# Modulation vectors of a diffusion backbone: partition sums by VectorE and one fold per sweep, where TensorE summed every batch

## The chip, the cores and the metric

The kernel runs on one core of a Trainium2 chip. A core has a matrix engine (TensorE, PE in the profile), a vector engine (VectorE, DVE), a scalar engine (ScalarE, ACT), GpSimd (POOL) and SyncE (SP), which here issues all loads and stores. PEld is TensorE's loading of weights. The metric is the time on the device in microseconds, the median of several runs.

## What is computed

Two layers of a diffusion backbone over 512 latent tokens and 256 context tokens of width 1024, all in fp32. Every sub-layer is modulated by vectors made from the conditioning inputs `c` and `c_ctx`:

```
sc, scc = silu(c), silu(c_ctx)
for i in range(2):
    m  = split(sc  @ w_mod[i] + b_mod[i], 9)      # w_mod[i]: 1024 x 9216
    mc = split(scc @ w_mod[i] + b_mod[i], 9)
    h = h + 0.5 * m[2] * swiglu(modulate(rmsnorm(h), m[0], m[1]), w1, w3, w2)      # ffn1, D_FF = 2816
    n = modulate(rmsnorm(h), m[3], m[4])
    h = h + m[5] * token_mixing(n, ...)            # pooling, latent attention, differential attention
    h = h + 0.5 * m[8] * swiglu(modulate(rmsnorm(h), m[6], m[7]), w1, w3, w2)      # ffn2
    # the context stream hc likewise with mc (its mixing and ffn2 in the first layer alone)
return rmsnorm(h)
```

## The kernel before

**Sweeps.** All large matmuls run in "sweeps" of units (`plan_sweeps`). A unit has two slots s = 0, 1; each slot is one 128-column tile of weights, split by ACT (`hi_w`, L811) and DVE (`lo_w`, L1070, `split_lo`) into a high and a low part, and three matmuls per 128-row tile of the input (hi x hi, hi x lo, lo x hi, L563) over 768 tokens, in pieces of 512 and 256. An `_up` sweep has 11 units over 8 input tiles (w1 in slot 0, w3 in slot 1), a `_down` sweep 4 units over 11 input tiles. Each feed-forward part is up, down, up, down (arg 0, 0, 1, 1); between ffn1 and ffn2 stand five `in` sweeps, the mixer and an `out` sweep. Each slot has one buffer for its raw, high and low weights, so DVE can split the next weights of a slot only when PE has finished the slot's last unit (`unit_done`); PE waits for `lo_ready`. At the start of an `_up` sweep with arg 0 and of the first `in` sweep (`starts_norm`) the normed input is made tile by tile by DVE and ACT (`norm_x`), and PE runs both slots of unit 0 together as the tiles come.

**Modulation vectors.** The first 16 tiles of 128 modulation columns are made by PE in the prologue. The other 128 are made beside the feed-forward sweeps: one *batch* of two tiles (`MOD_T`) per unit, in the eight up and down sweeps of layer 0 and in the first down sweep of layer 1 (11 or 4 batches each, 64 in all). SP loads 1 MB of `w_mod` per batch into `mod_w` (`load_mod`, after the last batch's sums). DVE (`mod_add`, L1165) multiplies each of the 8 row tiles of 256 columns by one value of silu(c) per partition, for c and for c_ctx, and adds them up in `mod_acc` (128 x 512, two streams of 256): 2 TENSOR_SCALAR (L1175) and 14 SCALAR_TENSOR_TENSOR (L1178). What is left is a sum over the 128 partitions. PE does it (`mod_tiles`, L569): four matmuls per batch with a 128 x 128 part of `mod_acc` as weights and a tile of ones as the moving side, into `pair[2]` in PSUM, after every unit. DVE takes one column of each of the results, adds the bias and writes `mod` (`mod_evict`, L1182, two instructions of 2 columns at L1188) in the next pass. `gate` (L1358) and the shift and scale of the norms are read from `mod`.

**Order.** It is written out by hand: each engine has one stream of instructions, and semaphores join them. In one pass of an up loop DVE runs: split slot 0, product of slots 0 and 1 (L1141) and its low part (L1144), split slot 1, evict, next batch. PE runs slot 0, slot 1, `mod_tiles`.

## Time and profile before

| | us |
|---|---|
| time, median of 3 runs | 3199.53 (3188.82 to 3199.97) |
| profiled execution: span from first to last instruction | 3194.2 |
| PE busy | 3027.5 (95%) |
| DVE busy | 1519.1 (48%) |
| ACT busy | 875.4 (27%) |
| share of the chain that ended last: PE / DVE / ACT | 88% / 5% / 4% |

The files of this kernel give the span of the profiled execution and the times of three runs; no time beside the span is listed for the profiled execution itself. The median of the runs is 5.3 us above the span. The chain is followed back from the last instruction: at each step to what released it, or to the instruction before it on its engine. Of the page, the chain says what bounds the kernel and the groups by line say what an operation takes; the timelines give the order in a stretch, with the idle time before an instruction in brackets and what ended it. Ends of matmuls are modelled, so the step from one start to the next is the better measure of their pace. PE clock is given as a share of 2.4 GHz; it has two levels, 1.2 and 2.4 GHz.

### The profile page before, as it was taken

How to read it: one execution, taken by the hardware profiler on the slowest of the kernel's cores; microseconds unless marked ns; L12 is line 12 of the kernel's file. 1: busy time of each engine (PE TensorE's matmuls, PEld its weight loads, DVE VectorE, ACT ScalarE, POOL GpSimd, SP SyncE). 2: the span in 40 equal slices, each digit the busy share in tenths (PEclk: the TensorE clock that was granted, in tenths of full speed). 3: DMA queues.
4: the chain of work that ended last, by engine and by line, in shares of the span. 5: the costliest groups of instructions: out<-in, count | busy, mean ns of one | idle time of the engine just before them, and what ended most of it. 6: DMA issues, size and time to landing. Idle time of an engine off the chain costs nothing.

```text
span 3194.2 us, 41772 instructions
## 1 busy us (share of the span) xinstructions
PE 3027.5 (95%) x16066; PEld 2495.7 (78%) x16066; DVE 1519.1 (48%) x2542; ACT 875.4 (27%) x1174; POOL 109.1 (3%) x82
## 2 busy tenths in 40 slices
PE   7999999989879889999999899999989889899998
PEld 3888888878647578888888788888868647678886
DVE  4665465541377447555565523422242376443333
ACT  3221121131346732111121312112131246432222
POOL 0000000000340000000000000000000230000000
PEclk9999999999999999999999999999999989999999
DMA  5434334312200023442433122312213200123332
GB/s 187 125 112 131 101 112 132 98 41 66 59 0 1 6 68 106 124 123 89 124 117 114 40 66 82 96 57 61 70 48 74 65 1 1 58 74 103 88 99 72
DMA packets 421951, 254.62 MB, mean 80 GB/s; under 512 B 25729, under 2 KB 417513, under 8 KB 421866
## 3 DMA queue, kind: packets, MB, share of 16 engines
q1 hardware_dynamic: 421866, 253.46, 26.7%
q8 instruction: 57, 0.93, 0.1%
q14 instruction: 28, 0.23, 0.0%
HBM read 251.34 MB, written 2.10 MB: 79 GB/s over the span
## 4 chain that ended last, share of the span: by engine, by line
PE 88%; DVE 5%; ACT 4%; issue 2%; DMA 0%; SPq 0%; DVEq 0%; ACTq 0%
PE pair L563 76%; PE pair L671 3%; PE pair L743 2%; PE pair L576 2%; PE pair L692 1%; PE pair L497 1%; DVE buf L1123 1%; PE pair L675 1%; ACT buf L957 1%; DVE n_lo L1114 1%; DVE proj L1234 1%; ACT L830 1%; PE pair L654 1%; DVE buf L1233 0%; DMA pro_w<-in_w_mod 0%
## 5 line engine op out<-in xcount | busy, mean ns | idle before, releaser
L563 PE MATMUL pair<-n_hi,hi_w 128*128 128x512 f32 (+1 forms) x3224 | 911.8, 352 | 51.7 <-DVE n_lo L1114 42.7
L563 PE MATMUL pair<-n_lo,hi_w 128*128 128x512 f32 (+1 forms) x3224 | 905.4, 350 | 0.0
L563 PE MATMUL pair<-n_hi,lo_w 128*128 128x512 f32 (+1 forms) x3224 | 904.0, 349 | 0.0
L563 PEld LDWEIGHTS pair<-n_hi,hi_w 128*128 128x128 f32 x3224 | 516.3, 190 | 141.6 <-issue 49.2
L1070 DVE TENSOR_TENSOR lo_w<-raw_w,hi_w 128x1024 fp32r<-128x1024 f32 (+1 forms) x296 | 387.9, 1311 | 484.3 <-ACT hi_w L811 480.4
L563 PEld LDWEIGHTS pair<-n_hi,lo_w 128*128 128x128 f32 x3224 | 515.9, 189 | 87.0
L563 PEld LDWEIGHTS pair<-n_lo,hi_w 128*128 128x128 f32 x3224 | 516.2, 190 | 86.5 <-issue 0.2
L811 ACT CAST hi_w<-raw_w 128x1024 fp32r<-128x1024 f32 (+1 forms) x296 | 329.0, 1112 | 406.3 <-PE pair L563 402.7
L1178 DVE SCALAR_TENSOR_TENSOR mod_acc<-mod_w,silu_c,mod_acc 128x256 f32<-128x256 f32 x896 | 360.4, 483 | 0.0
L563 PE MATMUL pair<-h_hi,hi_w 128*128 128x512 f32 x1232 | 343.7, 349 | 0.0
L563 PE MATMUL pair<-h_lo,hi_w 128*128 128x512 f32 x1232 | 342.1, 347 | 0.0
L563 PE MATMUL pair<-h_hi,lo_w 128*128 128x512 f32 x1232 | 341.9, 347 | 0.0
L1141 DVE TENSOR_TENSOR buf<-pair,buf 128x768 f32<-128x768 f32 (+1 forms) x88 | 78.4, 891 | 404.8 <-PE pair L563 404.8
L1160 DVE SCALAR_TENSOR_TENSOR x<-pair,gate,x 128x512 f32 (+3 forms) x136 | 82.0, 638 | 351.6 <-PE pair L563 351.2
L866 ACT CAST h_hi<-buf 128x768 f32 (+3 forms) x88 | 68.9, 783 | 608.4 <-DVE buf L1141 608.4
L563 PEld LDWEIGHTS pair<-h_hi,lo_w 128*128 128x128 f32 x1232 | 195.2, 188 | 32.5
L563 PEld LDWEIGHTS pair<-h_lo,hi_w 128*128 128x128 f32 x1232 | 195.1, 188 | 32.5
L563 PEld LDWEIGHTS pair<-h_hi,hi_w 128*128 128x128 f32 x1232 | 195.1, 188 | 31.5
L862 ACT ACTIVATE buf<-pair 128x768 f32<-128x768 f32 (+1 forms) x88 | 66.8, 759 | 475.0 <-PE pair L563 475.0
L823 ACT ACTIVATE buf<-x 128x768 f32 (+3 forms) x56 | 43.8, 784 | 375.1 <-DVE x L1160 373.2
L1282 DVE TENSOR_REDUCE neg_max<-pair 128x1 f32<-128x768 f32 (+1 forms) x120 | 101.7, 850 | 88.0 <-PE pair L675 54.0
L957 ACT ACTIVATE buf<-pair,neg_max 128x768 f32<-128x768 f32 (+1 forms) x120 | 97.0, 811 | 125.9 <-PE pair L692 66.0
(157 smaller groups left out, 1940.9 us busy)
## 6 DMA issues: line engine op xcount, KB each, us to landing
raw_w<-in_ffn_w SPq DMA_DIRECT2D x176, 512.0 KB, 3.7
mod_w<-in_w_mod SPq DMA_DIRECT2D x64, 1024.0 KB, 5.0
raw_w<-in_ffn_w SPq DMA_DIRECT2D x64, 704.0 KB, 4.6
raw_w<-in_w_in SPq DMA_DIRECT2D x38, 512.0 KB, 3.8
pro_w<-in_w_mod SPq DMA_DIRECT2D x2, 4096.0 KB, 19.0
raw_w<-in_w_out SPq DMA_DIRECT2D x16, 512.0 KB, 3.8
x_tok<-in_x SPq DMA_DIRECT2D x4, 512.0 KB, 5.4
out<-x_tok SPq DMA_DIRECT2D x4, 512.0 KB, 2.7
```

What stands on the lines that cost most here:

```text
L563: mm = pe.matmul(pair[s][:, a:a + m], wt[:, k * P:(k + 1) * P], tile(src, k, m, a), start=(n == 0 and wt is hi and src is src_hi), stop=(n ...
L576: mm = pe.matmul(pair[2][:, (2 * m + e) * P:(2 * m + e + 1) * P], mod_acc[:, e * MOD_W + m * P:e * MOD_W + (m + 1) * P], ones[:, :], start ...
L671: mm = pe.matmul(pair[s][:, a:a + m], tile(proj, T_DQ + h, P, q0), tile(k_odd, h, m, k0 + a) if s else tile(proj, T_DK + h, m, k0 + a), st ...
L811: act.copy(hi_w[s][:, 0:w["kt"] * P], raw_w[s][:, 0:w["kt"] * P]).then_inc(hi_ready[s], 1)
L862: act.activation(act_buf[:, 0:width(w, 0)], pair[0][:, 0:width(w, 0)], ACT.Silu)\
L866: act.copy(tile(h_hi, i, width(w, 1)), hid_buf[:, 0:width(w, 1)]).then_inc(hhi_ready, 1)
L957: act.activation(buf[step_buf(L, n) + (s if kind == "diff" else 0)][:, 0:nk], pair[s][:, 0:nk], ACT.Exp, bias=neg_max[:, c % 8:c % 8 + 1], ...
L1070: dve.tensor_tensor(lo_w[s][:, 0:m], raw_w[s][:, 0:m], hi_w[s][:, 0:m].bitcast(F32), ALU.subtract)\
L1141: dve.tensor_tensor(hid_buf[:, 0:m], pair[1][:, 0:m], act_buf[:, 0:m], ALU.mult)\
L1160: ins = dve.scalar_tensor_tensor(out=xs, in0=pair[s][:, a:a + m], scalar=gate[:, bass.ds((2 * i + s) * 2 + e, 1)], in1=xs, op0=ALU.mult, o ...
L1178: ins = dve.scalar_tensor_tensor(out=acc, in0=part, scalar=gain, in1=acc, op0=ALU.mult, op1=ALU.add)
L1282: dve.tensor_reduce(neg_max[:, c:c + 1], pair[s][:, 0:nk], AX.X, ALU.max, negate=True)\
```

## The change

The sum over partitions is made in two steps. After each batch DVE reduces `mod_acc` with one `tensor_reduce` that transposes blocks of 32 x 32 as it reads (`apply_transpose`): within each group of 32 partitions every column is summed, and column 32 j + q of the 512 lands in partition q of the group, column j of 16, in `mod_part`. The four groups are added by PE once per sweep (`mod_fold`): `fold` holds four 32 x 32 unit matrices on top of each other and is the weight tile of four matmuls, whose moving side is every fourth column of `mod_part` (44 columns after an up sweep, 16 after a down sweep) and whose outputs go to partitions 0, 32, 64 and 96 of `pair[2]`. The fold of a sweep stands in the next sweep, behind slot 0 of its unit 0, or behind both slots where the sweep starts with a norm. DVE's evict is one pair of instructions per sweep, at the same place, ahead of that sweep's first batch; `gate` is made behind it. `mod_part` has two buffers, used in turn. Four small loads on SP fill `fold`, ahead of the two prologue loads of `w_mod`. Nine folds take the place of 64 times four matmuls.

```diff
@@ SP @@
+            for g in range(4):
+                sp.dma_start(fold[32 * g:32 * (g + 1), :], t["k_ident"][0:32, 0:32]).then_inc(fold_full, 16)
@@ PE @@
-            def mod_tiles(w, i):
-                b = cnt["batch"] + i
-                pe.wait_ge(mod_sum, 2 * KD * b)
-                pe.wait_ge(mod_out, b)
-                for m in range(MOD_T):
-                    for e in range(2):
-                        mm = pe.matmul(pair[2][:, (2 * m + e) * P:(2 * m + e + 1) * P],
-                                       mod_acc[:, e * MOD_W + m * P:e * MOD_W + (m + 1) * P], ones[:, :],
-                                       start=True, stop=True)
-                mm.then_inc(mod_done, 1)
+            def mod_fold(w):
+                pe.wait_ge(fold_full, 16 * 4)
+                pe.wait_ge(mod_folded, cnt["batch"])
+                pe.wait_ge(mod_out, cnt["mod"])
+                n = w["n"]
+                for j in range(4):
+                    mm = pe.matmul(pair[2][32 * j:32 * (j + 1), 0:2 * MOD_T * n], fold[:, :],
+                                   mod_part[cnt["mod"] % 2][:, j:8 * MOD_T * n:4], start=True, stop=True)
+                mm.then_inc(mod_done, 1)
+                cnt["mod"] += 1
-            def sweep(w):
-                per = mod_tile(w) is not None
+            def sweep(w, before):
                 if starts_norm(w):
                     unit(w, 0, (0, 1), True)
                 else:
                     unit(w, 0, (0,), True)
+                if before is not None and mod_tile(before) is not None:
+                    mod_fold(before)
+                if not starts_norm(w):
                     unit(w, 0, (1,), True)
-                if per:
-                    mod_tiles(w, 0)
                 if w["n"] > 1:
                     with pe.Fori(1, w["n"]) as i:
                         unit(w, i, (0,), False)
                         unit(w, i, (1,), False)
-                        if per:
-                            mod_tiles(w, i)
@@ DVE @@
             def mod_add(w, i):
...
-                dve.wait_ge(mod_done, b)
+                    dve.wait_ge(mod_folded, b)
...
+                dve.wait_ge(mod_sum, 2 * KD * (b + 1))
+                at = i * (8 * MOD_T)
+                dve.tensor_reduce(mod_part[cnt["mod"] % 2][:, bass.ds(at, 8 * MOD_T)],
+                                  mod_acc[:, :].rearrange("p (j f) -> p j f", f=32), AX.X, ALU.add,
+                                  apply_transpose=True).then_inc(mod_folded, 1)
-            def mod_evict(w, i):
...
+            def mod_evict(w):
+                n, u = w["n"], mod_tile(w)
+                dve.wait_ge(mod_done, cnt["mod"] + 1)
...
+                for e in range(2):
+                    ins = dve.tensor_tensor(cols_of[:, :, :, e], sums[:, :, e, :], bias, ALU.add)
                 ins.then_inc(mod_out, 1)
             def sweep(q):
...
                 if not starts_norm(w):
                     split_lo(w, 0, 1)
+                if q and mod_tile(SWEEPS[q - 1]) is not None:
+                    mod_evict(SWEEPS[q - 1])
+                if w["arg"] == 0 and w["what"] in ("ffn1_down", "ffn2_down", "out"):
+                    make_gate(w)
                 if ends_step(w):
                     clear_x()
                 if per:
                     mod_add(w, 0)
                 finish(w, 0, 0)
                 if w["n"] > 1:
                     with dve.Fori(1, w["n"]) as i:
...
                         if per:
-                            mod_evict(w, i - 1)
                             mod_add(w, i)
```

On DVE, at the hand-over from the first up sweep to the first down sweep of layer 0, the kernel before has (a row is a line, operation, output <- inputs and shape; brackets name the semaphores it waits for):

```order
L1070 TENSOR_TENSOR lo_w<-raw_w,hi_w 128x1408 [waits hi_ready0]
L1141 TENSOR_TENSOR buf<-pair,buf 128x768 [waits h_ready,pair_free0,unit_done1]
L1144 TENSOR_TENSOR h_lo<-buf,h_hi 128x768 [waits hhi_ready]
L1188 TENSOR_SCALAR mod<-pair,b_mod 128x2 [waits mod_done]
L1188 TENSOR_SCALAR mod<-pair,b_mod 128x2
L1358 TENSOR_SCALAR gate<-mod 128x16 [waits mod_out]
L1070 TENSOR_TENSOR lo_w<-raw_w,hi_w 128x1408 [waits hi_ready1,dve_chain]
L1175 TENSOR_SCALAR mod_acc<-mod_w,silu_c 128x256 [waits mod_done,mod_full]
L1175 TENSOR_SCALAR mod_acc<-mod_w,silu_c 128x256
L1178 SCALAR_TENSOR_TENSOR mod_acc<-mod_w,silu_c,mod_acc 128x256 [waits mod_sum] x14
L1160 SCALAR_TENSOR_TENSOR x<-pair,gate,x 128x512 [waits unit_done0]
L1160 SCALAR_TENSOR_TENSOR x<-pair,gate,x 128x256
```

The changed kernel has there, with its own line numbers (4 to 20 higher):

```order
L1148 TENSOR_TENSOR h_lo<-buf,h_hi 128x768 [waits hhi_ready]
L1074 TENSOR_TENSOR lo_w<-raw_w,hi_w 128x1408 [waits hi_ready1]
L1202 TENSOR_TENSOR mod<-pair,b_mod 128x22 [waits mod_done]
L1202 TENSOR_TENSOR mod<-pair,b_mod 128x22
L1209 TENSOR_SCALAR gate<-mod 128x16 [waits mod_out]
L1180 TENSOR_SCALAR mod_acc<-mod_w,silu_c 128x256 [waits mod_folded,mod_full,dve_chain]
L1180 TENSOR_SCALAR mod_acc<-mod_w,silu_c 128x256
L1183 SCALAR_TENSOR_TENSOR mod_acc<-mod_w,silu_c,mod_acc 128x256 [waits mod_sum] x14
L1189 TENSOR_REDUCE mod_part<-mod_acc 128x16 [waits mod_sum]
L1164 SCALAR_TENSOR_TENSOR x<-pair,gate,x 128x512 [waits unit_done0]
L1164 SCALAR_TENSOR_TENSOR x<-pair,gate,x 128x256
```

The evict and the gate have moved from ahead of the weight split to behind it, and the `mod_done` that they wait for is now that of PE's fold in this sweep; the reduction stands behind the batch.

On PE, at the end of the loop body of the first up sweep, the kernel before has

```order
L563 MATMUL pair<-n_hi,lo_w 128x512
L563 MATMUL pair<-n_hi,lo_w 128x256
L572 REGISTER_ALU
L576 MATMUL pair<-ones,mod_acc 128x128 [waits mod_out,mod_sum]
L576 MATMUL pair<-ones,mod_acc 128x128 x3
L591 REGISTER_ALU
L591 COMPARE_AND_BRANCH
```

and the changed kernel, first there and then between slot 0 and slot 1 of unit 0 of the first down sweep:

```order
L569 MATMUL pair<-n_hi,lo_w 128x512
L569 MATMUL pair<-n_hi,lo_w 128x256
L597 REGISTER_ALU
L597 COMPARE_AND_BRANCH
```

```order
L569 MATMUL pair<-h_hi,lo_w 128x512
L569 MATMUL pair<-h_hi,lo_w 128x256
L582 MATMUL pair<-mod_part,fold 32x44 [waits mod_out,mod_folded,fold_full]
L582 MATMUL pair<-mod_part,fold 32x44 x3
L569 MATMUL pair<-h_hi,hi_w 128x512 [waits h_ready,pair_free1,lo_ready1]
```

The four matmuls of every pass are gone, and four with 32 output partitions stand once between the two slots.

## Rows read from the trace of the kernel before

**Rows 1.** The page's chain that ended last, shares by engine.

```profile
PE 88%; DVE 5%; ACT 4%; issue 2%; DMA 0%; SPq 0%; DVEq 0%; ACTq 0%
```

**Rows 2.** The chain in order of time (start us, us, what): an up and a down pass.

```profile
121.76 0.89 PE pair L576 x8
122.65 16.96 PE pair L563 x96
...
558.56 23.32 PE pair L563 x132
```

**Rows 3.** The same view: first up sweep of layer 1, which makes no vectors.

```profile
1813.26 194.68 PE pair L563 x1092
```

**Rows 4.** Timeline (start us, us, engine, line, what, count [idle before]): one up pass.

```profile
108.13 0.34 DVE L1188 TENSOR_SCALAR mod<-pair,b_mod 128x2 f32 x2
...
121.59 1.05 PE L576 MATMUL pair<-ones,mod_acc 128*128 128x128 f32 x8
121.88 0.96 DVE L1141 TENSOR_TENSOR buf<-pair,buf 128x768 f32<-128x768 f32 x1 [5.56 <-PE pair L563]
```

**Rows 5.** Groups by line: records, busy us, mean ns, idle before.

```profile
L576 PE MATMUL pair<-ones,mod_acc 128*128 128x128 f32 x512 | 67.6, 275 | 2.6 <-DVE mod_acc L1178 2.6
```

**Rows 6.** Timeline of DVE: last update of x ahead of the mixer's norm.

```profile
654.53 1.14 DVE L1160 SCALAR_TENSOR_TENSOR x<-pair,gate,x 128x512 f32<-128x512 f32 x2 [6.17 <-PE pair L563]
```

**Rows 7.** Timeline of PE: eight small transposes of the prologue.

```profile
58.82 0.65 PE L505 MATMUL pair<-ident,mod_rows 2*128 2x2 f32 x8 [0.72 <-DVE mod_rows L1096]
```

**Rows 8.** Timeline of PE in the mixer: weights of 128 and of 64 columns.

```profile
1013.02 1.50 PE L743 MATMUL pair<-proj,v_tok 128*128 128x128 f32 x12
1014.36 1.46 PE L675 MATMUL pair<-proj 96*128 96x512 f32 x4
...
1022.65 1.52 PE L743 MATMUL pair<-proj,v_mla 128*64 128x128 f32 x12
1024.10 1.56 PE L675 MATMUL pair<-proj 96*128 96x512 f32 x4
```

**Rows 9.** Groups by line with shapes kept apart: reductions on DVE.

```profile
L1282 DVE TENSOR_REDUCE neg_max<-pair 128x1 f32<-128x768 f32 x96 | 91.5, 957 | 77.1 <-PE pair L675 45.1 <-PE pair L671 31.9
L1282 DVE TENSOR_REDUCE neg_max<-pair 128x1 f32<-128x256 f32 x24 | 10.1, 422 | 10.9 <-PE pair L675 8.9 <-PE pair L671 1.5
```

**Rows 10.** Timeline of DVE: start of the first down sweep.

```profile
269.43 0.61 DVE L1175 TENSOR_SCALAR mod_acc<-mod_w,silu_c 128x256 f32<-128x256 f32 x2
269.96 5.63 DVE L1178 SCALAR_TENSOR_TENSOR mod_acc<-mod_w,silu_c,mod_acc 128x256 f32<-128x256 f32 x14
277.11 1.14 DVE L1160 SCALAR_TENSOR_TENSOR x<-pair,gate,x 128x512 f32<-128x512 f32 x2 [1.52 <-PE pair L563]
278.52 1.63 DVE L1070 TENSOR_TENSOR lo_w<-raw_w,hi_w 128x1408 fp32r<-128x1408 f32 x1 [0.27 <-ACT hi_w L811]
```

**Rows 11.** Timelines of DVE, then PE: first up sweep, behind its norm.

```profile
79.88 5.63 DVE L1178 SCALAR_TENSOR_TENSOR mod_acc<-mod_w,silu_c,mod_acc 128x256 f32<-128x256 f32 x14
85.42 1.22 DVE L1070 TENSOR_TENSOR lo_w<-raw_w,hi_w 128x1024 fp32r<-128x1024 f32 x1
...
85.56 1.16 PE L576 MATMUL pair<-ones,mod_acc 128*128 128x128 f32 x8 [1.41 <-DVE mod_acc L1178]
86.69 0.62 PE L563 MATMUL pair<-n_hi,hi_w 128*128 128x512 f32 x2
```

**Rows 12.** PE timeline behind the mixer's norm; busy times of 688:690 (PEclk fourth figure).

```profile
686.89 0.61 PE L563 MATMUL pair<-n_hi,hi_w 128*128 128x512 f32 x2 [2.04 <-DVE lo_w L1070]
...
690.99 0.52 PE L563 MATMUL pair<-n_lo,hi_w 128*128 128x512 f32 x2
...
688.00:690.00 2.00, 2.00 (x8) 0.50 0.93 257
```

**Rows 13.** Timeline of SP's queue; busy times of 10:11 (last two: DMA share, GB/s).

```profile
10.66 0.25 SPq L363 DMA_DIRECT2D lam_row<-in_diff_lambda  x1
...
10.00:11.00 1.00, 0.00 (x0) 1.00 1.00 410
```

## What I predict

> **What bounds the kernel now.** I read the chain that ended last first, then the same chain in order of time, then the timelines of TensorE (PE) and VectorE (DVE) where one sweep hands over to the next. PE holds 88% of the chain [rows 1], so a PE instruction inside a sweep costs its full pace. The chain in order of time says so directly: in an up sweep the 96 matmuls of one loop pass take 16.96 us, then the eight L576 records take 0.89 us, then the next pass starts; a down pass is 23.32 us with the same 0.89 us behind it [rows 2]. (An fp32 matmul leaves two records, so 8 records are the four matmuls of a batch.) What a pass costs without them is in the same kernel: the first up sweep of layer 1 makes no modulation vectors, and its 1092 records run as one piece of 194.68 us [rows 3], which is 17.1 us per 96, a few slow ones at its start included. So nothing else is waiting right behind PE there: without L576 a pass of 16.96 us is to be had. DVE has room: after its last weight split in an up pass it sits idle for 5.56 us until PE ends its unit [rows 4].
>
> **The matmuls that go.** L576 has 512 records [rows 5], 8 per batch, so 64 batches. Not all lie on the path. The last batch of a `_down` sweep with arg 1 in layer 0 (two of them) is followed by a norm, which hangs on DVE and ScalarE (ACT); DVE's last update of x there starts when L563 ends, not when L576 does [rows 6], so nothing is gained. The first batch of the two sweeps that begin with a norm and make vectors (the first up sweep, and `ffn2_up` arg 0 of layer 0) is costed below from its own rows. The other 60 are on the path: 60 x 0.89 = **53.4 us gained**.
>
> **The folds that come.** Nine, one per sweep with batches, each four matmuls with 32 weight columns and 44 or 16 moving columns, 8 records. Two of them (at the start of `in` arg 0 of layer 0 and of the first up sweep of layer 1) fall where PE is idle anyway; seven are on the path. No such matmul is in the trace. From above: 8 full-size records, 0.89 us [rows 2]. From below: PE's smallest fp32 work, eight transposes, takes 0.65 us [rows 7]; less is possible if the four overlap, down to about 0.3, half of that, by estimate. On top, PE changes from a 128-column to a 32-column layout and back. The nearest rows are 12 records with 64-column weights, which take 1.45 us from their start to the next group's where the same 12 with 128 columns take 1.34 [rows 8]: 0.11 for a change, 0.22 for both. I take 0.65 + 0.22 = 0.9 us, near the smallest work because the moving side is short; the range is 0.3 to 1.2. **7 x 0.9 = 6.3 us back** (2.1 to 8.4).
>
> The Trainium skill speaks against the change here: "TensorEngine Tiling (Array Packing)", Key Properties, says that changing the tiling mode drains TensorE. The same section says that tiles can load and multiply in parallel. The rows show only the 0.11 us for a change to 64 columns; if the drain were hidden and the four tiles ran at once the folds would cost about 2 us in place of 6.3.
>
> **The new reduction on DVE.** Each batch gets one TENSOR_REDUCE of 128x512 to 128x16 that transposes 32x32 blocks as it reads. Plain reductions take 957 ns for 768 columns and 422 for 256 [rows 9], so 1.045 ns a column and 0.69 us for 512. A transposing one is not in the trace. From below the 0.42 us of 256 columns; from above twice the slope plus the fixed part, about 1.3, and I keep 2.0 as the far bound. I take 0.69, since the number of columns read is what the rows scale with. In the loop it is free: the old evict of two instructions (0.34 us) goes [rows 4], and 5.56 us of idle time cover the rest.
>
> The Trainium skill, "Vector Engine (DVE) Microarchitecture Reference", section 3.8, says of the transposing front end that it is "pipelined to sustain one element per cycle per lane", which would leave 0.69 as it is. "VectorE: DVE Perf Modes", in its closing table, calls tensor_reduce the slowest DVE op on a hot path. No row here shows it transposing.
>
> **Sweep starts: a new wait on DVE.** In a sweep that follows one with batches, DVE now waits for PE's fold, which stands after slot 0 of unit 0, and only then makes its first batch. Queued behind that wait are the batch, the x update in a down sweep, and the split of slot 0's next weights, for which PE waits after slot 1. Before, the batch ran under slot 0. Worked out from the moment the fold ends: 0.28 us until DVE starts (L1141 starts at 121.88, PE's unit had ended at 121.6, where L576 starts [rows 4]), evict 0.34, the batch from its first to its last instruction 6.15 (269.43 to 275.59 [rows 10]), the reduction with its wait 0.75, then
> - up sweeps (two in layer 0): split 1.22 [rows 11]. Sum 8.7 us against slot 1's 16.96 / 2 = 8.48: PE is late by about 0.25, **0.5 us for both**.
> - down sweeps (four): x update 1.14 and split 1.63 [rows 10], gate and waits 0.3. Sum 10.6 against 23.32 / 2 = 11.66: **0**, with 1 us to spare, less where x_sum is cleared first. With a reduction of 2 us the ups would be late by 1.6 each and the downs by 0.3 to 1.
>
> SyncE's load of the next modulation weights waits for the same batch, so it is issued later by about one unit, and so is the batch that needs it. The fifth down sweep with batches, that of layer 1, has no fold ahead and stays as it is; the up sweep behind it has a fold and no batch, so nothing is queued there but the evict.
>
> **The two norm starts with a batch.** PE waited until the batch was summed, ran L576 from 85.56 and resumed at 86.69, with DVE's split running beside it [rows 11]. Now PE resumes after batch, reduction and split: 79.88 + 5.63 = 85.51, + 0.75, + 1.22 = 87.5 us, that is 0.8 later. At the second place DVE has a little more cover; with 0.5 there, by estimate, **1.3 us come back.** PE is now idle for some 3 us there, where it had been idle 1.41 us before a filler. Where this kernel leaves PE idle for 2.04 us before a resumption, the granted clock is at half (0.50 of full, 1.2 in place of 2.4 GHz) soon after: from 686.89 to 690.99 seven groups of two matmuls take 4.10 us in place of 7 x 0.353 = 2.47 [rows 12, 2]. So I add 1.6 us at both places: **3.2 us back.**
>
> **The two norm starts with a fold.** PE's 2.04 us of idle time [rows 12] now holds the fold. But DVE's evict waits for it and stands ahead of the weight split that PE waits for. PE stops at 684.85 (686.89 - 2.04), so the fold ends at 685.7, and with 0.28 + 0.34 DVE is free at 686.3; the split began at 686.89 - 0.05 - 1.22 = 685.6. With the fold queued close behind the last unit I take **0.6 each, 1.2 us back.** I leave the clock as it was there.
>
> **Four small loads at the start** of `fold` stand ahead of the two 4 MB loads on SP's queue. An issue of such a load is 0.25 + 0.05 us, four make 1.2 us at most. The DMA engines were busy for all of that time (share 1.00 from 10 to 11 us) [rows 13], so most of it is hidden behind the queue; between 0 and 1.2 I take **0.6 us back**.
>
> **Sum.** 53.4 - 6.3 - 0.5 - 1.3 - 3.2 - 1.2 - 0.6 = 40.3 us. The profiled execution spans 3194.2 us; the median of the runs, 3199.53, is 5.3 us above, about what lies around the span. 3194.2 - 40.3 = 3153.9 in the profile, and 3199.5 - 40.3 = **3159.2 us** as time.
>
> **Rivals.**
> - *The handovers cost more.* The reduction takes 2 us and the clock also falls at the ups and at two of the downs. Up starts +2 x 1.3, norm starts +2 x 1.3, downs +4 x 0.6, four more falls of the clock +6.4, folds at 1.2 us +2.1, loads +0.6: 16.7 us, so 3176. For it: DVE at an up start is late already by my sum. Against: a PE wait of 1.41 us did not bring the clock down. Chance 0.14.
> - *They cost less.* Folds at 0.3 us (-4.2), no fall of the clock at the norm starts with a fold because the fold breaks up the idle time (-3.2), none from the loads (-0.6): 3151. Chance 0.18.
> - *The other side: the transposing reduction is slow.* Its place is every up pass (40 inside the loops). The cover is 5.56 us plus the 0.34 of the old evict less the 0.89 by which the pass shortens, so it decides from about 5 to 5.5 us; below that only the starts pay. With R us the loss is 40 x (R - 5.5) in the loops and 8 x (R - 0.7) at starts, if all of them pay; it outruns the gain of 40 by another 0.5% (16 us) at R = 5.9. At R = 7 it is 60 + 50 us: 3269. For it: no row shows a transposing read. Against: 5.9 us would be eleven times the slope of plain reductions. Chance 0.03.
> - *The gain is taken by another wait*, so that the change doesn't buy what the removed matmuls cost: the 1 MB load per batch comes later than the shorter passes ask for and DVE, then PE, wait for it, by 0.5 us or more of the 0.89 in each of some 60 passes: about 3190. Against: traffic has room, and the sweep without batches runs at the full pace. Chance 0.05.
>
> **How the numbers follow.** Forecast 0.60 (3150 to 3170), cheaper handovers 0.18, dearer 0.14, gain taken 0.05, slower 0.03. A difference of under 0.5% (16 us) is what a measurement of this kernel can't tell from none; only the last two cases fall short of it. Faster 0.92, same 0.05, slower 0.03. The range takes in both handover cases and, below, that the three runs themselves reach 10.7 us under their median: 3142 to 3177.
>
> **What the new profile would show.** Chain in order of time: up passes of 16.96 us back to back with no piece between (right), or a short DVE piece in each (reduction too slow). The group of the fold: 72 records, the step over it about 0.9 us. The reduction's own mean, 0.7 us. DVE's wait for PE before the evict at seven starts, near 10 us or less each, and at up starts a PE wait for lo_w of 0.2 to 0.5 us. At the two norm starts with a batch PE resumes some 3 us after it stopped and at half clock. If the time is above 3177, one of these is off by several times its size.

## The result, and the profile after

| | before | changed |
|---|---|---|
| time, median (us) | 3199.11 | 3138.28 |
| runs | 4 | 4, 3134.65 to 3144.0 |
| span of the profiled execution (us) | 3194.2 | 3134.9, its time 3136.8 |

The ratio is 0.9819, 95% interval 0.9801 to 0.9837: 61 us less. The forecast was 3159.2 us with a range of 3142 to 3177, so the direction was right and the time lies 3.7 us below the range. Span against span, 59.3 us went where 40.3 were expected. (What lies around the span is 3136.8 - 3134.9 = 1.9 us, not the 5.3 that the prediction put down to it; the profiled execution of before was a little under its median. The forecast was counted from the median, so this shifts nothing.) The other 19 us are what this part of the document looks for.

The page's chain that ended last, and from the groups by line and the table of waits the two new operations and DVE's new wait (waits: us in total, times, longest):

```profile
PE 86%; DVE 6%; ACT 4%; issue 2%; DMA 0%; SPq 0%; ACTq 0%; DVEq 0%
...
L582 PE MATMUL pair<-mod_part,fold 128*32 128x16 f32 (+1 forms) x72 | 2.7, 221 | 0.0
...
L1189 DVE TRANSPOSE_TENSOR_REDUCE mod_part<-mod_acc 128x512 f32 (+1 forms) x64 | 45.6, 712 | 8.5 <-DVE mod_acc L1183 4.7
...
DVE mod L1202 <- PE pair L582: 56.4, 9, 7.2
```

Against [rows 1] the picture is the same, PE a little less and DVE a little more. The 512 records of L576 [rows 5] are gone; 72 of L582 stand in their place. The reduction takes 0.712 us, where 0.69 was predicted from plain reductions [rows 9].

Now DVE's timeline in the first up sweep (start us, us, line, what), to be read against [rows 4], where L1141 was the same instruction as L1145 here:

```profile
106.69 0.96 DVE L1145 TENSOR_TENSOR buf<-pair,buf 128x768 f32<-128x768 f32 x1 [5.37 <-PE pair L569]
...
117.08 0.71 DVE L1189 TRANSPOSE_TENSOR_REDUCE mod_part<-mod_acc 128x512 f32 x1
...
123.44 0.96 DVE L1145 TENSOR_TENSOR buf<-pair,buf 128x768 f32<-128x768 f32 x1 [4.54 <-PE pair L569]
...
140.19 0.96 DVE L1145 TENSOR_TENSOR buf<-pair,buf 128x768 f32<-128x768 f32 x1 [4.55 <-PE pair L569]
```

From one L1145 to the next is a pass: 16.75 us. A pass of before was 16.96 + 0.89 = 17.85 [rows 2]. So 1.10 us went per pass, and not 0.89: the 96 matmuls themselves take 0.21 us less than they did. No edit touches them. That is the first sign of what the prediction lacked, and the second is in the last part of the kernel, where no vectors are made at all. There the granted clock is full, PE is never idle, and the number of matmul records in 100 us (in brackets) is a direct reading of their pace. First the kernel before, then the changed one:

```profile
2950.00:3050.00 100.00, 100.00 (x430) 1.00 0.30 86
```

```profile
2950.00:3050.00 100.00, 100.00 (x438) 1.00 0.34 99
```

430 and 438 records of 512 columns: 233 and 229 ns each. The new program runs old instructions faster.

### The profile page after: what moved, and what is told of

Read it like the earlier page. It is cut to its first block, busy times and chain, and to the rows that moved or that the text cites. A ratio compares the mean times of both kernels' runs of the same rounds, so it can differ in the third digit from the quotient of the medians.

```text
span 3134.9 us, 40610 instructions
## 1 busy us (share of the span) xinstructions
PE 2957.6 (94%) x15626; PEld 2440.8 (78%) x15626; DVE 1538.9 (49%) x2496; ACT 874.9 (28%) x1174; POOL 108.5 (3%) x82
## 4 chain that ended last, share of the span: by engine, by line
PE 86%; DVE 6%; ACT 4%; issue 2%; DMA 0%; SPq 0%; ACTq 0%; DVEq 0%
PE pair L569 77%; PE pair L675 3%; PE pair L747 2%; PE pair L696 1%; PE pair L503 1%; PE pair L679 1%; DVE buf L1127 1%; ACT buf L961 1%; DVE n_lo L1118 1%; ACT L834 1%; DVE mod_acc L1183 1%; DVE proj L1255 1%; PE pair L658 1%; DVE buf L1254 1%; ACT L837 0%
## 5 line engine op out<-in xcount | busy, mean ns | idle before, releaser
L569 PE MATMUL pair<-n_hi,hi_w 128*128 128x512 f32 (+1 forms) x3224 | 903.5, 350 | 57.3 <-DVE n_lo L1118 42.7
L569 PE MATMUL pair<-n_lo,hi_w 128*128 128x512 f32 (+1 forms) x3224 | 901.8, 349 | 0.0
L569 PE MATMUL pair<-n_hi,lo_w 128*128 128x512 f32 (+1 forms) x3224 | 897.5, 347 | 0.0
L569 PEld LDWEIGHTS pair<-n_hi,hi_w 128*128 128x128 f32 x3224 | 515.2, 190 | 143.7 <-issue 51.8
L569 PEld LDWEIGHTS pair<-n_lo,hi_w 128*128 128x128 f32 x3224 | 518.6, 190 | 82.8 <-issue 0.2
L569 PEld LDWEIGHTS pair<-n_hi,lo_w 128*128 128x128 f32 x3224 | 515.6, 189 | 82.1
L569 PE MATMUL pair<-h_hi,hi_w 128*128 128x512 f32 x1232 | 341.4, 347 | 2.2 <-DVE lo_w L1074 2.2
L569 PE MATMUL pair<-h_lo,hi_w 128*128 128x512 f32 x1232 | 341.3, 346 | 0.0
L569 PE MATMUL pair<-h_hi,lo_w 128*128 128x512 f32 x1232 | 339.4, 345 | 0.0
L1145 DVE TENSOR_TENSOR buf<-pair,buf 128x768 f32<-128x768 f32 (+1 forms) x88 | 78.4, 891 | 356.6 <-PE pair L569 356.6
L569 PEld LDWEIGHTS pair<-h_lo,hi_w 128*128 128x128 f32 x1232 | 196.1, 188 | 31.6
L569 PEld LDWEIGHTS pair<-h_hi,hi_w 128*128 128x128 f32 x1232 | 194.8, 188 | 33.0 <-issue 2.8
L569 PEld LDWEIGHTS pair<-h_hi,lo_w 128*128 128x128 f32 x1232 | 195.0, 188 | 31.4
```

Of the source, the lines that this page charges most:

```text
L569: mm = pe.matmul(pair[s][:, a:a + m], wt[:, k * P:(k + 1) * P], tile(src, k, m, a), start=(n == 0 and wt is hi and src is src_hi), stop=(n ...
L1145: dve.tensor_tensor(hid_buf[:, 0:m], pair[1][:, 0:m], act_buf[:, 0:m], ALU.mult)\
```

## Experiments: chance or address

"Pace" is here the step from the start of one large matmul, or of one pair, to the next. Two theories for its change. **Chance**: an execution of any of these programs falls into one pace or the other. **Address**: the change puts `fold`, 32 columns of fp32 or 128 bytes, into SBUF behind `ones`, and everything allocated behind it lies 128 bytes higher, the moving operands `n_hi`, `n_lo`, `h_hi` and `h_lo` too. `n_hi` began at byte 112192 of its partition, and begins at 112320 in the changed kernel. The weights (`hi_w`, `lo_w`) and `x` are allocated ahead of `fold` and stay where they were. (The expectations name a third theory, **code**: where the matmul stream is disturbed decides the pace. The runs on addresses below test it too, since they leave every instruction as it is.)

The two programs once more, unedited (before_again, after_again):

> The kernel before, unchanged, profiled once more. It asks whether the pace of the large matmuls is a property of the program or of the single execution. In the first profile of the kernel before every sweep steps at 353.3 ns per pair (a piece of 512 and one of 256 columns) and at 233.2 ns per 512-column matmul in the last sweeps; in the changed kernel some sweeps step at 349 ns and the last ones at 228.8 ns. Theory ADDRESS (the buffer of 32 columns moved all later buffers) and theory CODE (where TensorE's stream is disturbed decides which of two paces it falls into): 353.3 and 233.2 again, ratio 1.000. Theory CHANCE (an execution falls into one pace or the other): some sweeps at 349 or 228.8 ns, and a time between 3185 and 3200 us.

Measured: 3198.92 us (ratio 1.0006, interval 0.9995 to 1.0016), the slow pace in every sweep.

> The changed kernel, unchanged, profiled once more. Theories ADDRESS and CODE: the same pattern of paces by sweep as in its first profile (349 ns per pair in the first up and down sweep, in the `in` sweeps and in two up sweeps of layer 0, 228.8 ns in the last sweeps), ratio 0.981. Theory CHANCE: another pattern; the time moves with it by up to 10 us.

Measured: 3138.92 us (ratio 0.9815, 0.9798 to 0.9832); the fast pace again wherever only 512 columns are computed. In the sweeps of 512 and 256 columns the pattern was another one: from its first matmul to that of the next sweep, the second up sweep of layer 0 took 184.85 us where the first execution had 186.84, and the third 193.95 where it had 191.86. There chance does have a part, and this was not expected by the theory of addresses as it was written down.

Then the addresses alone. In the kernel before, one line more, a buffer that nothing uses (before_shift):

```diff
         ones = sb("ones", P)
+        gap = sb("gap", 32)
         mod = sb("mod", DEPTH * UNITS_MOD * 2)
```

> The kernel before with one unused buffer of 32 columns where the change puts its fold matrix, so that every later buffer lies at the addresses of the changed kernel; nothing else differs. Theory ADDRESS: the last sweeps step at 228.8 ns and some earlier ones at 349 ns per pair, and the time falls by 9 to 20 us, ratio 0.994 to 0.997. Theories CODE and CHANCE: no systematic difference from before, ratio 1.000 within 0.002.

Measured: 3180.11 us (ratio 0.9942, 0.9924 to 0.996). Some 16.6 us for a line that computes nothing. And in the changed kernel, the shift taken out while everything else stays (after_noshift):

```diff
-        fold = sb("fold", 32)
         mod = sb("mod", DEPTH * UNITS_MOD * 2)
...
         h_lo = sb("h_lo", FG * TOK, F32R)
+        fold = sb("fold", 32)
```

> The changed kernel with the fold matrix allocated behind all other buffers, so that these lie where they lay before. Theory ADDRESS: every sweep steps at 353.3 and 233.2 ns as before, and the time is 3138 + 19 = 3157 us, ratio 0.987. Theories CODE and CHANCE: 3138 us within 5, ratio 0.981, with sweeps at 349 and 228.8 ns.

Measured: 3153.45 us (ratio 0.9861, 0.9844 to 0.9878), inside the predicted range. Every sweep is back at the slow pace. Two rows of DVE's timeline, one pass apart, and the count of the last part:

```profile
125.18 0.96 DVE L1145 TENSOR_TENSOR buf<-pair,buf 128x768 f32<-128x768 f32 x1 [4.76 <-PE pair L569]
142.14 0.96 DVE L1145 TENSOR_TENSOR buf<-pair,buf 128x768 f32<-128x768 f32 x1 [4.77 <-PE pair L569]
```

```profile
2950.00:3050.00 100.00, 100.00 (x431) 1.00 0.32 93
```

The pass is 16.96 us, exactly what [rows 2] promised. So chance and code are out as the cause of the difference between the two programs, and the change has two parts: the announced one, worth 43.3 us (3196.75, measured beside it, to 3153.45), and one that nobody intended, the move of the buffers, worth 14.5 us (3153.45 to 3138.92). By the sweeps' lengths in the two profiled executions, 6.7 of the 16.8 us between them lie in sweeps of 512 columns alone, where the pace follows the address every time; nearly all of the rest lies in the other sweeps, where it does not.

**Whose address?** In shift_h `fold` stands between `n_lo` and the buffers behind it, so that only `h_hi`, `h_lo` (and `proj`) are moved:

```diff
         n_lo = sb("n_lo", KD * TOK, F32R)
+        fold = sb("fold", 32)
```

> The changed kernel with `fold` placed between `n_lo` and the buffers behind it: `h_hi` and `h_lo` (moving operands of the down sweeps) and `proj` lie 128 bytes higher than before the change, as in the changed kernel; `n_hi`, `n_lo` (moving operands of the up, in and out sweeps), `rstd`, `buf0` to `buf3` and the small vectors lie as before the change. Theory, each matmul's pace goes by the address of its own moving operand: in layer 1 the two ffn2 down sweeps step at 228.8 ns and the ffn2 up and out sweeps at 233.2; of the 16 us that the full shift brought here only 2 to 6 us come, 3147 to 3151.5 us. Rival A, one of the buffers in front (the outputs or inputs of DVE and ACT) matters: then no sweep is faster, 3153.5 us. Rival B, the pace of all sweeps hangs on something that h_hi, h_lo or proj share: all at 228.8, near 3138 us.

Measured: 3154.51 us (ratio 0.9867, 0.9851 to 0.9884), 3 us above the range that was expected. The pace answers the question better than the time does. Records in 50 us of the first ffn2 down sweep of layer 1 (moving operands `h_hi`, `h_lo`), first after_noshift, then this kernel:

```profile
2886.00:2936.00 50.00, 50.00 (x216) 1.00 0.31 91
```

```profile
2886.50:2936.50 50.00, 50.00 (x220) 1.00 0.32 93
```

and of this kernel 100 us of the up sweep behind it (moving `n_hi`, `n_lo`), with the same columns:

```profile
2950.00:3050.00 100.00, 100.00 (x430) 1.00 0.31 90
```

The down sweep took the fast pace and the up sweep did not. So for the down sweeps it is the address of `h_hi` and `h_lo` that counts, and `rstd`, the vectors and the other buffers in front of `n_hi`, which stayed, have no part in it; nor does it matter where the up sweep's results are written, since it writes `h_hi` and `h_lo` and stayed slow. For the up sweeps no run moves `n_hi` and `n_lo` without the buffers in front of them, so that it is their own moving operand there too is likely, but not shown. Since the weights never moved, the address itself and the distance from the weights can't be told apart either.

**Which addresses?** More unused columns behind `fold`, in the changed kernel: `gap = sb("gap", 16)` in gap16, 48 in gap48.

> The changed kernel with an unused buffer of 16 columns behind `fold`: everything from `mod` on lies 192 bytes higher than before the change (the changed kernel: 128). The start of `n_hi` modulo 256 bytes was 64 before, is 192 in the changed kernel, and is 0 here. Theory, the pace gets better with the alignment of the moving operand's start: the 512-column sweeps step at 228.8 ns or less and all 768-column sweeps at the faster of their two paces (349 in place of 353.3 ns for a pair): 12 us under the changed kernel, near 3127 us. Rival, it is the address bit of 128 bytes, or distance to another buffer, and not alignment: the time is that of the changed kernel, 3138 us, or, where 192 is as bad as 0, 3153 us.

Measured: 3136.01 us (ratio 0.9811, 0.9794 to 0.9827).

> The changed kernel with 48 unused columns behind `fold`: `n_hi` and the other moving operands start at 128 modulo 256 bytes (before the change 64, changed kernel 192, with 16 columns 0). Theory A, the distance to the next 256-byte boundary matters through the middle of the three paces that were seen: as 0, a step of 232.2 ns in the 512-column sweeps and 350.9 a pair in the others, 3136 us. Theory B, the address bit of 128 decides: as in the changed kernel 228.8 ns, 3138 us or less. Theory C: as before the change, 233.2 and 353.3 ns, 3153 us.

Measured: 3130.6 us (ratio 0.9785, 0.9769 to 0.98). The same 100 us in both:

```profile
2950.00:3050.00 100.00, 100.00 (x432) 1.00 0.34 98
```

```profile
2950.00:3050.00 100.00, 100.00 (x443) 1.00 0.35 102
```

| start of the moving operands modulo 256 bytes | 64 (before) | 0 (16 columns) | 192 (changed kernel) | 128 (48 columns) |
|---|---|---|---|---|
| ns a step, 512-column matmuls | 233.3 | 232.4 | 228.9 | 226.7 |
| time, changed kernel (us) | 3153.5 | 3136.0 | 3138.3, 3138.9 | 3130.6 |

The steps are the length of the last up sweep of layer 1 (123.20, 122.69, 120.85 and 119.68 us) by its 528 records. My theory for gap16, that rounder alignment is better, fell: 0 is the second slowest in the 512-column sweeps. Of gap48's three theories B comes nearest: the two starts in the upper half of 256 bytes, 128 and 192, are the quick ones, and 0 and 64 the slow ones; but it is not the same pace within a half. Four starts are too few for a rule. In the 768-column sweeps things are less simple. A pass of an up sweep is 48 pairs of matmuls (512 and 256 columns), so its length gives the pair. With a start at 0 it is 16.85 us, 351 ns a pair, and with 64 it is 16.96, 353 ns, in every sweep. With 192 it is 16.96 or 16.75 (349 ns), and which of them differs from execution to execution of one program. Here are two passes of the second up sweep of layer 0 in the changed kernel, and two in after_again:

```profile
435.07 0.96 DVE L1145 TENSOR_TENSOR buf<-pair,buf 128x768 f32<-128x768 f32 x1 [4.74 <-PE pair L569]
452.03 0.96 DVE L1145 TENSOR_TENSOR buf<-pair,buf 128x768 f32<-128x768 f32 x1 [4.74 <-PE pair L569]
```

```profile
419.55 0.96 DVE L1145 TENSOR_TENSOR buf<-pair,buf 128x768 f32<-128x768 f32 x1 [4.53 <-PE pair L569]
436.30 0.96 DVE L1145 TENSOR_TENSOR buf<-pair,buf 128x768 f32<-128x768 f32 x1 [4.53 <-PE pair L569]
```

16.96 us a pass in one and 16.75 in the other. (At 128 both 16.96 and 16.64 occur.) In every one of these traces the pace holds from a sweep's third pass to its end, and wherever it changes, a wait or other matmuls (a fold, or L576 in before_shift) stand in between. What picks it stays open, as does why an address matters at all. The Trainium skill, "SBUF — State Buffer", section "Operand start alignment", asks only that an operand starts at a multiple of its element size, and says of its own measurements that "these runs timed nothing"; all four starts here obey it, and they differ by 6.6 ns of 233.

## Experiments: how near was the slow reduction

The rival on the other side had a rule: from a reduction of 5.5 us on every up pass pays. In reduce10, made from after_noshift, each batch's reduction is done nine times more, into an unused buffer:

```diff
+                for a in range(9):
+                    dve.tensor_reduce(again[:, a * 8 * MOD_T:(a + 1) * 8 * MOD_T],
+                                      mod_acc[:, :].rearrange("p (j f) -> p j f", f=32), AX.X, ALU.add,
+                                      apply_transpose=True)
                 at = i * (8 * MOD_T)
```

> The changed kernel with `fold` placed behind `h_lo` (3153.5 us), and each batch's reduction done ten times, nine of them into an unused buffer: the modulation vectors are unchanged, DVE gets 9 x 0.711 = 6.4 us more per batch. This tests the rival of the slow reduction: R = 7.1 us. By the prediction's rule the loops lose 40 x (7.1 - 5.5) = 64 us and the starts up to 8 x 6.4 = 51 us: 3153.5 + 64 + 51 = 3269 us at most; if the starts with little to lose (down sweeps, 23.3 us a pass) hide half of theirs, near 3240 us. If DVE's slack in an up pass is what the profile of the changed kernel shows, 4.55 us, the loops lose 40 x 1.8 = 74 us. Rival: DVE's time is not what limits there (semaphores and loads do): the time moves by less than 20 us.

Measured: 3230.55 us (ratio 1.0104, 1.0087 to 1.0121), 77 us more than without. One pass of DVE's timeline:

```profile
170.53 5.63 DVE L1184 SCALAR_TENSOR_TENSOR mod_acc<-mod_w,silu_c,mod_acc 128x256 f32<-128x256 f32 x14
176.20 5.46 DVE L1190 TRANSPOSE_TENSOR_REDUCE again<-mod_acc 128x16 f32<-128x512 f32 x9
181.58 0.67 DVE L1194 TRANSPOSE_TENSOR_REDUCE mod_part<-mod_acc 128x512 f32 x1
182.17 1.19 DVE L1075 TENSOR_TENSOR lo_w<-raw_w,hi_w 128x1024 fp32r<-128x1024 f32 x1
183.41 0.96 DVE L1146 TENSOR_TENSOR buf<-pair,buf 128x768 f32<-128x768 f32 x1
```

L1146 has no idle time in front of it any more: DVE is the bound. The ten reductions take 176.20 to 182.25, 6.05 us and not 7.1, because each starts a little before the one ahead has ended (0.60 us each; the tenth at 181.58, the nine until 181.66). The instruction L1146 before this one starts at 165.92, so the pass is 183.41 - 165.92 = 17.49 us, 0.53 over PE's 16.96 (the passes alternate between 17.35 and about 17.5 to 17.6), and so the point from which a pass pays is 6.05 - 0.53 = 5.5 us by estimate, the figure of the prediction. With R = 6.05 its rule gives 40 x 0.55 + 8 x 5.35 = 65 us; 77 were measured. Most of the missing part is in the down sweeps' loops, which the rule held to be free. They lose 10 us, nearly all of it in the second pass (25.69 us in the first down sweep, where after_noshift has 23.32), since what is late at the start is still late there; the third and fourth take 23.32 again in that sweep. With R = 7.1 instead of the measured 6.05 both numbers of the expectation came out too high.

## Experiments: the handovers

PE's timeline, in the changed kernel, at the start of the first down sweep with arg 1, with DVE's and ACT's steps that lead up to it:

```profile
555.77 0.71 DVE L1189 TRANSPOSE_TENSOR_REDUCE mod_part<-mod_acc 128x16 f32<-128x512 f32 x1
...
556.40 1.10 DVE L1164 SCALAR_TENSOR_TENSOR x<-pair,gate,x 128x512 f32<-128x512 f32 x2
...
557.54 0.85 ACT L827 ACTIVATE buf<-x 128x768 f32<-128x768 f32 x1 [17.69 <-DVE x L1164]
...
558.29 1.36 ACT L815 CAST hi_w<-raw_w 128x1408 fp32r<-128x1408 f32 x1
...
559.68 1.63 DVE L1074 TENSOR_TENSOR lo_w<-raw_w,hi_w 128x1408 fp32r<-128x1408 f32 x1 [2.17 <-ACT hi_w L815]
...
561.55 0.59 PE L569 MATMUL pair<-h_hi,hi_w 128*128 128x512 f32 x2 [1.20 <-DVE lo_w L1074]
```

Read it backwards. PE waits 1.20 us for `lo_w`, DVE's split waits 2.17 us for `hi_w`, and ACT makes `hi_w` only at 558.29 because in its program the square of x stands ahead of it, which waits for DVE's x update, which stands behind the batch, which stands behind the fold. If that is so, putting the batch back ahead of the wait must remove it (order_fix; `late` is whether a fold is due; `dst` names the half of `mod_part`):

```diff
-                if q and mod_tile(SWEEPS[q - 1]) is not None:
+                late = q and mod_tile(SWEEPS[q - 1]) is not None
+                if per:
+                    mod_add(w, 0, (cnt["mod"] + bool(late)) % 2)
+                if late:
                     mod_evict(SWEEPS[q - 1])
...
                 if ends_step(w):
                     clear_x()
-                if per:
-                    mod_add(w, 0)
```

> The changed kernel with `fold` placed behind `h_lo` (so that all other buffers lie where they lay before the change; that kernel took 3153.5 us), and with one more edit: at a sweep's start DVE makes the sweep's first batch ahead of its wait for the fold, not behind it. Theory: at the start of the two down sweeps with arg 1 of layer 0 PE was idle 1.3 us each, because x update, its square on ACT and the split that ACT has behind it all stood behind DVE's batch, and the batch behind the fold. With the batch under slot 0 again these two waits go: 2.6 us less, 3150.9 us, and the matmuls keep their slow pace (233.2 ns a step in the 512-column sweeps). Rival: these waits have another cause (the reduction's own 0.71 us, or ACT's order alone): then they stay and the time stays at 3153.5.

Measured: 3153.36 us (ratio 0.9862, 0.9843 to 0.9881), no gain in the median. In its trace both waits are gone: from the first matmul of such a sweep to that of the next takes 104.92 us, against 106.24 and 106.20 in after_noshift, 2.6 us for the two, the price predicted. The profiled execution itself took 3150.68 us, where 3150.9 was expected, but that is luck: the four executions reach from 3147.42 to 3157.39, and other stretches of the profiled one differ by more than the effect, both ways. One of them is the clock at another place. PE resumes behind the mixer's norm in `in` arg 0 of layer 0 after the same wait in both kernels. In after_noshift the clock stays up (first fence; the granted clock of a stretch is the figure behind POOL's), in order_fix it falls (second fence):

```profile
668.11 0.61 PE L569 MATMUL pair<-n_hi,hi_w 128*128 128x512 f32 x2 [1.84 <-DVE lo_w L1074]
...
668.00:670.00 2.00, 1.89 (x11) 1.67 (x12) 2.00 (x3) 0.00 (x0) 0.00 (x0) 1.00 0.28 60
```

```profile
666.89 0.61 PE L569 MATMUL pair<-n_hi,hi_w 128*128 128x512 f32 x2 [1.84 <-DVE lo_w L1074]
...
667.00:669.00 2.00, 2.00 (x9) 1.73 (x10) 1.84 (x2) 0.00 (x0) 0.00 (x0) 0.78 0.38 93
```

PE's idle time ahead of both is 1.84 us. That sweep takes 37.6 us in one and 40.6 in the other. It is not the edit that does this: the changed kernel and after_again are one program, the wait there is 1.85 and 1.84 us, and the clock fell to half in the first (39.65 us for the sweep) and stayed at full in the second (37.62). Differences of this kind are as large as the effect sought, so the time neither shows nor denies it, and only the wait itself in the trace does. What made the median no better stays open, since the other three executions left no trace.

Two kernels, v3_gap16 and v3_shift128, then also tried to shorten the starts behind a norm. In the two such sweeps with batches each batch is made one pass later, so that DVE's split goes first (the last batch falls into the next sweep's start); where a norm start has a fold, the evict goes behind the split:

```diff
+                if behind:
+                    v = SWEEPS[q - 1]
+                    mod_add(v, v["n"] - 1, None, cnt["batch"] - 1)
...
                         split_lo(w, i, 0)
+                        if late and starts_norm(w) and i0 == 1:
+                            mod_evict(SWEEPS[q - 1])
...
-                        if per:
+                        if late_batches(w):
+                            mod_add(w, 0 if i0 == 1 else i - 1)
+                        elif per:
                             mod_add(w, i)
```

> The kernel with 16 unused columns behind `fold` (3136.0 us), with the handovers put in another order: (1) a sweep's first batch again stands ahead of DVE's wait for the fold; (2) in the two sweeps that begin with a norm and make vectors every batch is made one loop pass later, so that DVE's first weight split there stands ahead of the first batch (the last batch is made at the start of the next sweep, and the loads of the modulation weights move by a pass too); (3) where a sweep begins with a norm and has a fold, DVE's evict stands behind that split. Theory: (1) takes the two waits of 1.3 us at the down starts with arg 1, 2.6 us; (2) takes 3.3 us of idle PE down to the 1.4 of before, 3.8 us at both, and with it the half clock that follows, 1.6 us each; (3) some 0.3 us at each of two places. Sum 10 us, near 3126 us. Rival: the clock falls after the shorter waits as well (it did at some norm starts with 2.3 us of idle PE and not at others), and then 3 us less are gained, 3129 us. Rival: the later loads or the batch that now stands ahead of the fold in the next down sweep make PE wait there; then the gain is under 4 us or a loss.

Measured: 3134.44 us (ratio 0.9798, 0.9784 to 0.9812), 1.6 us under gap16, where 10 were expected.

> The same new order of the handovers, without the 16 unused columns: buffers at the addresses of the changed kernel (its time 3138.3 and 3138.9 us; matmul steps of 228.8 ns in the 512-column sweeps, and 349 or 353.3 ns a pair in the others, by sweep and execution). Theory: 10 us under the changed kernel, near 3128.5 us, with more spread between executions than with the 16 columns, since its two paces are met by chance. Rival: the pace in a sweep is set by whether PE stalled at its start; with fewer stalls more sweeps, or fewer, run at the faster pace, and the time moves by up to 10 us more either way.

Measured: 3140.8 us (ratio 0.9811, 0.9795 to 0.9828), nothing gained. The trace of v3_gap16 shows the rival at work. PE's idle time behind the first norm did fall, from 2.93 us in gap16 to 2.04 (first row), but at the next down start DVE waits for the modulation weights and then PE for DVE:

```profile
85.98 0.62 PE L582 MATMUL pair<-n_hi,hi_w 128*128 128x512 f32 x2 [2.04 <-DVE lo_w L1087]
```

```profile
267.21 0.37 SPq L422 DMA_DIRECT2D mod_w<-in_w_mod  x1
...
272.25 0.61 DVE L1193 TENSOR_SCALAR mod_acc<-mod_w,silu_c 128x256 f32<-128x256 f32 x2 [3.34 <-DMA mod_w<-in_w_mod]
...
281.96 0.59 PE L582 MATMUL pair<-h_hi,hi_w 128*128 128x512 f32 x2 [1.80 <-DVE lo_w L1087]
```

There is one buffer `mod_w`. Two batches close together mean that the second one's 1 MB can be asked for only when the first is through with it, and it takes 5 us to come. Against gap16 the two norm sweeps got 1.3 and 3.6 us shorter and the down sweeps behind them 2.2 us longer each.

So the last kernel, order_gap48, keeps what worked: the batch ahead of the fold, the evict behind the split at norm starts, and the 48 unused columns.

> The kernel with 48 unused columns behind `fold` (3130.6 us, the best so far), with two of the three moves of the handovers, since the third (batches made a pass later) gained at the norm starts and lost as much at the next down starts: a sweep's first batch ahead of DVE's wait for the fold, and, where a sweep begins with a norm and has a fold, DVE's evict behind the first weight split. Theory: the waits of 1.5 and 1.3 us at the down starts with arg 1 go (2.8 us) and some 0.3 us at two norm starts; 3127.3 us. Rival: which pace a 768-column sweep takes at these addresses goes by how the sweep begins; then the time moves by up to some 5 us more either way, and 3130.6 is not beaten.

Measured: 3121.45 us (ratio 0.9763, 0.975 to 0.9777), the best of all, 17 us under the change as it was made. It came out 6 us lower than expected. In its trace the two waits are gone (104.71 us for each of those sweeps, 106.2 in gap48). Most of the rest is again pace: more 768-column sweeps at the fast one, among them the two up sweeps with arg 1 of layer 0, 183.59 us each where gap48 had 186.82 and 187.07, and `out` of layer 0 (77.94 for 79.20). The five runs reach from 3117.3 to 3125.5 us, so this is not one lucky execution, but whether the order of the handovers brings that pace about is not shown.

## Why the prediction was wrong, step by step

The pair before and after_noshift has equal addresses and equal paces, so it holds the change alone. Its spans differ by 3194.2 - 3151.7 = 42.5 us, and splitting them at the first matmul of each sweep gives a value for each step, with 0.89 us taken for every batch on the path. Each is one profiled execution against one:

| step | predicted (us) | measured (us) |
|---|---|---|
| 60 batches on the path | -53.4 | -53.4 |
| folds | +6.3 | +3.0 |
| up starts | +0.5 | 0 |
| down starts | 0 | +2.6 |
| norm starts with a batch, clock included | +4.5 | +5.7 |
| norm starts with a fold | +1.2 | -2.5 |
| loads at the start | +0.6 | +0.8 |
| mixers and other work that the change leaves alone | 0 | +1.2 |
| pace by address | not in the sum | 0 here; -16.8 in the changed kernel |

- **The step that failed** is none of these but one that was missing: the sum took the steps of all other matmuls as given. The change allocates a new buffer in front of the moving operands, and the buffer was costed only through its four loads. The move of the operands makes 3151.7 - 3134.9 = 16.8 us of span, and without it the time is 3153.45, inside the range and 5.8 us from the forecast. With the 2.2 us by which the steps above exceed the sum (42.5 for 40.3) that makes the 19 us. No rival of the prediction went below 3151 us; the range reached to 3142 only because the runs of before scatter, not by any mechanism. (Single executions of the two kernels differ by a few us in the mixers and in the clock too; by medians the move of the buffers is 14.5 us.)
- **That the other steps came within 2.2 us is in part luck.** Folds, up starts and norm starts with a fold came out 7.5 us better than predicted, the rest some 5 us worse, and of the first 2.5 us are the clock of one execution. The loads can't be read at all: from the first instruction to the first sweep it is 64.84 us in before and 65.65 in after_noshift, but 66.02 in before_again.
- **The matmuls that go** were right. L1145 follows itself by 16.96 us in after_noshift, L1141 of before by 17.85; the sweep without batches [rows 3] had shown this pass beforehand. The down sweep of layer 1, which has batches and no fold, went from 96.75 to 93.28 us, 4 x 0.87.
- **The folds** were sized at 0.9 us each and cost less than half of it. PE's timeline in the changed kernel:

```profile
268.29 0.51 PE L569 MATMUL pair<-h_hi,lo_w 128*128 128x512 f32 x2
268.73 0.34 PE L582 MATMUL pair<-mod_part,fold 128*32 128x44 f32 x8
269.00 0.50 PE L569 MATMUL pair<-h_hi,hi_w 128*128 128x512 f32 x1
```

  L569's next pair would have started at 268.64, since a pair takes 0.35 here, so the step costs 0.36; all folds on the path with 44 columns cost 0.36 to 0.37 in this trace and in after_noshift's, those with 16 columns 0.28. For seven that is 2.3 us. The 3.0 of the table comes from the lengths of the sweeps (9.34 us less in the second up sweep of layer 0 = 11 x 0.89 - 0.45), and what the other 0.1 us at each start are is not shown. The row taken was that of the transposes, with a change of layout on top; the moving columns alone would have given it, by estimate: eight records of 128 columns take 0.89 [rows 2], so eight of 44 take 0.31. The rule of the Trainium skill, "TensorEngine Tiling (Array Packing)", Key Properties, that changing the tiling mode drains TensorE can cost 0.1 us at most on the way in: 268.73 less 268.64. On the way back it lies inside the 0.27 us from the fold's start to that of L569 and can't be told apart. Whether the four tiles worked in parallel, as the section says they can, is not shown, since 0.31 is what one behind the other would take.
- **Up starts** were free. DVE at the first of them:

```profile
358.49 0.24 DVE L1202 TENSOR_TENSOR mod<-pair,b_mod 128x8 f32<-128x8 f32 x2 [6.23 <-PE pair L582]
...
365.47 1.18 DVE L1074 TENSOR_TENSOR lo_w<-raw_w,hi_w 128x1024 fp32r<-128x1024 f32 x1
```

  From the fold's end at 358.43 (it starts at 358.17 and takes 0.26) to the split's at 366.65 it is 8.22 us, where the sum had 8.7: its pieces overlap by some tenths, and 8.22 is inside slot 1's 8.48. PE does not wait there.
- **Down starts** were the weakest of the steps that it did cost. The prediction followed DVE to its split and called it hidden with 1 us to spare, and for the two with arg 0 that is right. At the two with arg 1 the path leaves DVE: x update, ACT's square, ACT's split, DVE's split, 1.3 us each. The prediction named what is queued behind the wait on DVE but not on ACT, which waits for DVE in turn; order_fix showed the cause.
- **Norm starts with a batch** were right in kind: PE idle 3.07 us where 3 was said, and half clock behind it. The changed kernel:

```profile
86.31 0.71 DVE L1189 TRANSPOSE_TENSOR_REDUCE mod_part<-mod_acc 128x16 f32<-128x512 f32 x1
86.94 1.18 DVE L1074 TENSOR_TENSOR lo_w<-raw_w,hi_w 128x1024 fp32r<-128x1024 f32 x1
...
88.18 1.01 PE L569 MATMUL pair<-n_hi,hi_w 128*128 128x512 f32 x2 [3.07 <-DVE lo_w L1074]
...
88.00:90.00 2.00, 1.82 (x5) 1.59 (x6) 0.99 (x2) 0.88 (x2) 0.00 (x0) 0.50 1.04 357
```

- **Norm starts with a fold** had a wait that isn't there. From the last matmul ahead of the mixer's norm to the first behind it, it is 2.31 us in before and in after_noshift alike, and 2.50 in both at the other such place. DVE, first before and then after_noshift:

```profile
685.61 1.23 DVE L1070 TENSOR_TENSOR lo_w<-raw_w,hi_w 128x1024 fp32r<-128x1024 f32 x1 [5.51 <-ACT hi_w L811]
```

```profile
666.33 0.24 DVE L1202 TENSOR_TENSOR mod<-pair,b_mod 128x8 f32<-128x8 f32 x2 [4.22 <-PE pair L582]
666.83 1.23 DVE L1074 TENSOR_TENSOR lo_w<-raw_w,hi_w 128x1024 fp32r<-128x1024 f32 x1 [0.26 <-ACT hi_w L815]
```

  The split waits for ACT's `hi_w` in both, and fold and evict are through before that comes: 0 where 0.6 was said, twice. The 2.5 us gained are the clock, which was left as in [rows 12] and varies there from execution to execution: it fell in before, the changed kernel and order_fix, and not in after_noshift and after_again.
- **The rivals.** "Cheaper handovers" was nearer for the folds (0.3) and would have come to 3151; it put the clock that doesn't fall down to the fold, but with a fold at that place it fell in some executions and not in others. The slow reduction's threshold held (5.5 us), and nothing of "the gain is taken by another wait" was seen.

## What to carry to other kernels

A new buffer can be an edit to every matmul whose operands lie behind it. Before a gain or loss of half a per cent is put down to the logic of a change, put the new buffer last and measure again, and when a kernel is done, try a few paddings: here 48 unused columns were worth 8 us and one idle line was worth 17. Where a wait is added on one engine, follow the queue behind it on the engines that wait for that engine, too.

## What the runs showed of the hardware that was not expected

- The step between 512-column fp32r matmuls at full clock depends on where the moving operands' buffers start: 233.3, 232.4, 228.9 and 226.7 ns for 64, 0, 192 and 128 modulo 256 bytes. The stationary operand did not move in any of these.
- In sweeps of 512- and 256-column pairs, at 128 and 192 two paces (353 ns a pair and 347 or 349) exist side by side in one program; each held from the third pass of a sweep to its end, and every change lay at a wait or at other matmuls. At 64 and 0 there was one pace, 353 and 351.
- A reduction over 128x512 fp32 that transposes 32x32 blocks takes 0.712 us alone and 0.60 in a row of ten; plain ones of 256 and 768 columns put a plain one of 512 at 0.69 by estimate.
- After equal waits of PE at the same place of one program, 1.85 and 1.84 us, the granted clock fell to half in one execution and stayed at full in another.
